# A transformer layer with gathered expert rows: the background work cut into one piece per pair of rows

## What is computed

```
def peer_ffn(hn, wq, subkeys, u, v):
    ...
        q = (xc @ wq).reshape(PEER_CHUNK, PEER_HEADS, 2, PEER_DKEY // 2)
        s = jnp.einsum('chpd,hpkd->chpk', q, subkeys).astype(jnp.float32)
        s1, i1 = lax.top_k(s[:, :, 0], PEER_TOPK)
        s2, i2 = lax.top_k(s[:, :, 1], PEER_TOPK)
        ...
        top, sel = lax.top_k(cand, PEER_TOPK)
        expert = jnp.take_along_axis(cidx, sel, axis=-1)
        g = jax.nn.softmax(top, axis=-1)
        act = jax.nn.gelu(jnp.einsum('cd,chkd->chk', xc, u[expert]).astype(jnp.float32))
        return jnp.einsum('chk,chkd->cd', (g * act).astype(v.dtype), v[expert])
```

## Time and profile before

| | us |
|---|---|
| three runs | 2373.06, 2374.31, 2378.94 |
| their median | 2374.31 |
| the profiled execution: its own time | 2377.95 |
| its span, first to last instruction | 2376.1 |
| of the span: up to the first gather | 722.7 |
| first dot to last dot | 728.8 to 2358.0 |
| mean granted clock of TensorE | 0.796 |

### The profile page before, as it was taken

How to read it: one execution, slowest core, us unless ns; L and a number is a source line. 1 busy time by engine, 2 the same in 40 slices (tenths; PEclk the granted TensorE clock), 3 DMA queues, 4 the chain that set the end, 5 groups by cost and what they waited for, 6 DMA issues and landing times. The chain is left out here.

```text
span 2376.1 us, 24181 instructions
## 1 busy us (share of the span) xinstructions
PE 1642.0 (69%) x8217; PEld 693.9 (29%) x8217; DVE 1360.5 (57%) x4295; ACT 403.7 (17%) x1217; POOL 650.6 (27%) x560
## 2 busy tenths in 40 slices
PE   5999998879794785786366566765664564655564
PEld 2334685535451221433021222431231111111111
DVE  2200026810217667456955675657776989999855
ACT  2000234612311220020101112101110100000101
POOL 0000000000005435423422343232443434444442
PEclk9999978989796897586678787667886757677777
DMA  7211600053009879878888997889999999999996
GB/s 217 71 42 64 205 11 1 3 186 124 36 1 377 355 297 410 354 289 310 316 343 325 381 390 318 354 333 360 393 381 418 396 381 351 395 395 385 391 385 278
DMA packets 124994, 654.73 MB, mean 276 GB/s; under 512 B 22960, under 2 KB 34256, under 8 KB 56928
## 3 DMA queue, kind: packets, MB, share of 16 engines
q0 software_dynamic: 78016, 562.07, 59.4%
q1 hardware_dynamic: 41816, 82.86, 10.2%
q10 hardware_dynamic: 5040, 8.26, 1.0%
HBM read 642.78 MB, written 14.55 MB: 277 GB/s over the span
## 5 line engine op out<-in xcount | busy, mean ns | idle before, releaser
L1362 PE MATMUL row_sum<-arena 64*64 64x512 f32 x4096 | 739.5, 852 | 587.2 <-DVE arena L2324 571.9
L767 POOL DMA_INDIRECT arena<-in_peer_uv,expert x512 | 594.0, 1160 | 1389.4 <-PE row_sum L1362 840.7
L2288 DVE CUSTOM_DVE_ANT_0 arena<-arena 128x1024 f32<-128x1024 f32 x520 | 637.0, 1225 | 333.4 <-DMA arena<-in_peer_uv,expert 322.1
L1362 PEld LDWEIGHTS row_sum<-arena 64*64 64x64 f32 x4096 | 174.3, 175 | 1110.3 <-DVE arena L2324 813.4
L1578 ACT ACTIVATE arena<-arena 128x2 f32<-128x2 f32 x260 | 53.2, 205 | 1135.9 <-DVE arena L2288 1135.3
L816 PE MATMUL bank<-arena 128*128 128x512 f32 (+2 forms) x288 | 119.9, 571 | 0.0
L1781 DVE TENSOR_TENSOR arena<-arena 128x256 f32<-128x256 f32 (+5 forms) x20 | 6.4, 320 | 197.3 <-ACT arena L1439 197.3
L816 PE MATMUL row_sum<-arena 128*128 128x512 f32 (+3 forms) x272 | 109.7, 558 | 0.0
L2307 DVE TENSOR_TENSOR arena<-arena 128x128 f32<-128x128 f32 x256 | 75.1, 293 | 8.4 <-DVE arena L2297 0.4
L1581 ACT ACTIVATE arena<-arena 128x2 f32<-128x2 f32 x260 | 53.3, 205 | 125.7 <-DVE arena L2294 125.6
L2324 DVE SCALAR_TENSOR_TENSOR arena<-arena 128x128 f32<-128x128 f32 x256 | 74.0, 289 | 0.1
(11 more groups left out here) (314 smaller groups left out, 2055.9 us busy)
## 6 DMA issues: line engine op xcount, KB each, us to landing
arena<-in_w_in SPq DMA_DIRECT2D x6, 2048.0 KB, 7.8
arena<-in_w_out SPq DMA_DIRECT2D x2, 4096.0 KB, 24.1
arena<-in_peer_uv,expert POOLq DMA_INDIRECT x512, 9.1
arena<-in_w_mq SPq DMA_DIRECT2D x2, 2048.0 KB, 12.6
arena<-in_peer_wq SPq DMA_DIRECT2D x2, 2048.0 KB, 11.2
arena<-in_w_mo SPq DMA_DIRECT2D x2, 2048.0 KB, 18.9
sc_scores<-arena ACTq DMA_DIRECT2D x4, 1024.0 KB
arena<-in_cache_mem_k SPq DMA_DIRECT2D x2, 2048.0 KB, 11.5
```

The costliest lines, as they stand in the source:

```text
L767: pool.indirect_dma_start(out=ring[k], out_offset=None, in_=a["peer_uv"], in_offset=bass.IndirectOffsetOnAxis(ap=idx, axis=0)).then_inc(ro ...
L1362: ins = pe.matmul(row_sum[r][o * HALF:(o + 1) * HALF, cols], spread[tokens, p % SPREADS, y, :], ring[k][tokens, D + half * 512:D + (half + ...
L2288: return dve.tensor_tensor_reduce(out=ring[k][:, 0:D], in0=ring[k][:, 0:D], in1=other, scale=1.0, scalar=0.0, op0=ALU.mult, op1=ALU.add, a ...
```

## The change

The generators stay, but every piece is given the number of the pair at which it is due, and all three engines call `advance(steps, p)` at each pair.

- On PE the background piece of pair p stands ahead of the value rows of pair p-1, no longer behind them.
- Pieces are cut smaller: one batch-and-group run of page keys per pair, two runs of page values, half a bank of the output projection, one query, one memory-key unit of the sample and so on. The halves of a page-key product and of a value product go to the two column halves of the array (`y`).
- Tile 3 and the sample tokens no longer share memory output, expert queries and scores: tile 3's end at pair 144, the sample's own memory attention follows, and its scores are made at pair 206. For that `w_mo` and the expert query weights `wq` are loaded once more each.
- The sample's eight heads are chosen as one, with (token, head) on 64 partitions, in group 27; the gates and expert numbers are brought into columns through DRAM and not by a transpose on PE.
- The gathers of the page values are issued one pair earlier and wait at pair 31; the retention state's four large DVE instructions are halved; three final norms move to the groups 17, 18 and 26.
- In the front only the order of the key scores changes (the two halves take turns).

The table of pairs and the core of the diff:

```diff
-VALUES_AT = 4
...
-FINAL_SQUARES = {PAIR_AT[H * t + 12, 7]: t for t in range(3)}
-FINAL_NORMS = {PAIR_AT[H * t + 13, 7]: t for t in range(3)}
-SAMPLE_HEADS_AT = 21
+FINAL_SQUARES = {PAIR_AT[n, 1]: t for t, n in enumerate((17, 18, 26))}
+FINAL_NORMS = {PAIR_AT[n, 5]: t for t, n in enumerate((17, 18, 26))}
+SAMPLE_HEADS_AT = 27
...
-    for head in range(H):
-        steps[SAMPLE_HEADS_AT + head].append((SAMPLE, head))
+    steps[SAMPLE_HEADS_AT].append((SAMPLE, 0))
...
-STEP_TURNS = ((1, 1), (2, 2), (3, 3), (4, 4), (5, 5), (6, 10), (7, 20), (8, 21), (9, 23), (10, 24), (11, 27),
-              (12, 28), (13, 29), (14, 30), (15, 35), (16, 38), (17, 39), (18, 42), (19, 44), (20, 45), (21, 46),
-              (22, 47), (23, 48), (24, 49), (25, 55), (26, 56), (27, 57), (28, 64), (29, 65), (30, 68), (31, 76),
-              (32, 77))
-STEPS_DONE = 99
+KEYS_AT, VALUES_AT, KIND_DONE = (14, 54), (41, 67), (51, 73)
+STATE_AT = 75
+OUT_AT = {PT - 1: 91, PT: 95}
+QUERIES_AT = 106
+UNITS_AT = 113
+MEM_OUT_AT = {PT - 1: 126, PT: 189}
+EXPERT_AT = {PT - 1: 134, PT: 196}
+MEM_KEYS_AT = (150, 162)
+MEM_VALUES_AT = (176, 184)
+NORM_COLS = 11
+STEPS_DONE = 999
...
+            sp.wait_ge(mo_done, 2 * PT)
+            sp.dma_start(back.wq, wq).then_inc(wq_in, 16)
+            sp.wait_ge(qp_done, 2 * H)
+            sp.dma_start(w_mo, w_mo_rows).then_inc(mo_in, 16)
+
+            sp.wait_ge(scores_stored, 16 * PT)
+            for piece, (s, v) in enumerate(((qp_done, 2 * H), (m_keyT_done, DB), (m_keyT_done, 2 * DB),
                                             (m_oT_done, PT * HM + 1))):
                 name, b0 = ("cache_mem_k", "cache_mem_v")[piece // 2], 4 * (piece % 2)
                 sp.wait_ge(s, v)
...
+                if t == SAMPLE:
+                    sp.wait_ge(gates_ready, 1)
+                    for dst, src in ((sc_expert, expert_p[0:64, :]), (sc_gate, best_v[0:64, 0:TOPK])):
+                        sp.dma_start(dst.rearrange("b (h k) -> (b h) k", h=H), src).then_inc(scratch_stored, 16)
+                    sp.wait_ge(scratch_stored, 96)
+                    sp.dma_start(expert_s[:, :], sc_expert.rearrange("b s -> s b"), allow_slow_non_contiguous=True).then_inc(idx_ready, 16)
+                    sp.dma_start(half_gate[:, SLOTS:SLOTS + DB], sc_gate.rearrange("b s -> s b"), allow_slow_non_contiguous=True).then_inc(sample_gates_in, 16)
...
-                    pool.wait_ge(idx_ready, 3)
+                    pool.wait_ge(idx_ready, 2 + 16)
                 else:
                     pool.wait_ge(routed, ROUTED[divmod(n, H)])
-                if (n, x) == (VALUES_AT, 0):
+                values_behind = 0 <= p - KEYS_AT[0] - BG - 1 < BG // 2
+                if p == KEYS_AT[0] + BG + 1:
                     pool.wait_ge(s_sc_done, 2)
                 for y in range(2):
                     nth, k = divmod(2 * p + y, RING)
@@ -771,8 +785,8 @@
...
-                    if n == VALUES_AT:
-                        gather_pages(val_rows, "cache_slc_v", val_in[0], 2 * x + y)
+                    if values_behind:
...
                     b = grp.out_bank(n)
                     bank = claim(b)
                     for k in range(KC):
-                        ins = pe.matmul(bank[:, 0:grp.width], grp.w_mq[:, k, hh * P:(hh + 1) * P], grp.hnT[:, k, :],
+                        if k == KC // 2:
+                            yield
+                        ins = pe.matmul(bank[0:R, :], grp.catT[t][:, k, 0:R],
+                                        grp.w_out[:, k, half * 512:(half + 1) * 512],
                                         start=(k == 0), stop=(k == KC - 1))
-                    ins.then_inc(qm_done, 1)
-                    freed[b] = (qm_ready, n + 1)
-                pe.wait_ge(qm_ready, HM * nth)
+                    ins.then_inc(out_done, 1)
+                    freed[b] = (out_added, n + 1)
+                    yield
+
+
+            def memory_query(grp, nth, hh):
+                n = HM * (nth - 1) + hh
...
+                            ins = pe.matmul(banks[2][y * 64:(y + 1) * 64, :], q_mask[0:HD, bg, :], keyT[0:HD, y, :],
+                                            start=(i == 0), stop=(i == len(runs) - 1))
                         return ins
 
-                    for i in range(BG * nc_):
-                        bg, cc = divmod(i, nc_)
-                        if i and i % 4 == 0:
-                            yield 5 + 3 * kind + i / (BG * nc_)
-                        bank = claim(gi % 2)
-                        for q in range(4):
-                            j = 4 * cc + q
-                            ins = pe.transpose(bank[0:HD, q * P:(q + 1) * P], keys[:, bg, j * HD:(j + 1) * HD], ident)
-                        ins.then_inc(s_keyT_done, 1)
-                        freed[gi % 2] = (s_keyT_ready, gi + 1)
+                    for i, run in enumerate(runs):
+                        yield KEYS_AT[kind] + i
                         if i:
-                            key_scores(i - 1, gi - 1)
-                        gi += 1
-                    key_scores(BG * nc_ - 1, gi - 1).then_inc(s_sc_done, 1)
-                    yield 6 + 3 * kind
-                    for cc in range(nc_):
-                        freed[2 + cc] = (s_max, 2 + kind)
+                            key_scores(i - 1)
+                        else:
+                            pe.wait_ge(qmask_ready, 1)
+                            pe.wait_ge(key_in[kind], (16 * BG, 16)[kind])
+                            claim(2)
+                        for y, (bg, j0) in enumerate(run):
+                            bank = claim(y)
+                            for q in range(4):
+                                j = j0 + q
+                                ins = pe.transpose(bank[0:HD, q * P:(q + 1) * P], keys[:, bg, j * HD:(j + 1) * HD], ident)
+                            ins.then_inc(s_keyT_done, 1)
+                            made += 1
+                            freed[y] = (s_keyT_ready, made)
+                    yield KEYS_AT[kind] + len(runs)
+                    key_scores(len(runs) - 1).then_inc(s_sc_done, 1)
+                    freed[2] = (s_max, 2 + kind)
...
-                    pe.wait_ge(val_in[kind], (16 * BG, 16)[kind])
-                    pe.wait_ge(s_pT_ready, 2 + kind)
-                    bank = claim(1)
+                    each = (2, 4)[kind]
                     for bg in range(BG):
-                        for j in range(nj):
-                            ins = pe.matmul(bank[0:HD, bg * R4:(bg + 1) * R4], vals[:, bg, j * HD:(j + 1) * HD],
-                                            s_probsT[:, j, bg * R4:(bg + 1) * R4], start=(j == 0), stop=(j == nj - 1))
+                        if bg % each == 0:
+                            yield VALUES_AT[kind] + bg // each
+                        if bg == 0:
+                            pe.wait_ge(val_in[kind], (16 * BG, 16)[kind])
+                            pe.wait_ge(s_pT_ready, 2 + kind)
+                            claim(1)
+                        for j in range(0, nj, 2):
+                            for y in range(2):
+                                ins = pe.matmul(banks[1][y * HD:(y + 1) * HD, bg * R4:(bg + 1) * R4],
...
+                                                vals[:, bg, (j + y) * HD:(j + y + 1) * HD],
+                                                s_probsT[:, j + y, bg * R4:(bg + 1) * R4], start=(j == 0), stop=(j == nj - 2))
                     ins.then_inc(s_oT_done, 1)
                     freed[1] = (s_oT_ready, 1 + kind)
+                    yield KIND_DONE[kind] - 1
...
+                cat_transposes(3)
+                out3, out_s = (output_projection(back, 2, t) for t in (3, SAMPLE))
+                for i in range(4):
+                    yield OUT_AT[3] + i
+                    next(out3)
+                    if i == 2:
+                        cat_transposes(SAMPLE)
+                for i in range(4):
...
+                yield from memory_rows(3, 2)
+                yield from expert_scores(3, 2)
...
-                key_scores_of(back, SAMPLE)
+                yield from memory_rows(SAMPLE, 3)
+                yield from expert_scores(SAMPLE, 3)
...
 
 
@@ -1379,15 +1434,9 @@
             for b in range(4, 8):
                 claim(b)
             for p, (n, x) in enumerate(PAIRS):
-                if (n, x) == (HEADS - 2, 2):
-                    bank = claim(0)
-                    pe.wait_ge(gates_ready, 1)
-                    pe.transpose(bank[:, 0:DB], expert_f[0:DB, :], ident[0:DB, 0:DB])
-                    pe.transpose(bank[:, DB:2 * DB], gate_t[0:DB, :], ident[0:DB, 0:DB]).then_inc(rt_done, 1)
+                advance(steps, p)
...
-
-            def sample_gates_shifted():
-
-                b3 = best_v[0:DB, :].rearrange("p (h k) -> p h k", h=H)
-                top = col[0:DB, 32:40]
-                order(dve.tensor_copy(top, b3[:, :, 0]))
-                tt(b3, b3, wide(top, DB, H, TOPK), ALU.subtract).then_inc(sample_gate, 1)
 
```

(16 more changed lines are left out.)

632 lines of the change are left out of this document (338 added, 294 removed).

## The result

The changed kernel takes 2287.46 us, the median of 4 runs (2273.87 to 2295.52); beside it the kernel before took 2376.62 us (2373.06 to 2379.31). The ratio is 0.962, 95% interval 0.957 to 0.967: 89 us less, where the prediction said 2276 us and 98 less. The profiled execution took 2289.83 us, its span is 2288.0.

A forecast was written before the change was run, and what follows sets the result against it. Bound: the gathers' bandwidth, with DMA idle behind large background pieces. Loop: gathers 1300, other traffic 134, jitter 49, PE's pieces 30, retention state 15, late loads 5, together 1533 us against 1631; hence 2276 us, range 2232 to 2335.

The forecast's parts named there:

- groups 21 to 28: Late pairs of the loop, sample's heads chosen at one go: 5.2 us a pair, DVE busy about 0.85.
- Late loads: Output weights asked for at about pair 85, wanted by PE at pair 91: 5 us (0 to 10).
- Page and window values: Value pieces on PE, 2.4 us each, 0.8 over the floor in 12 pairs: 10 us (0 to 20).
- The sample's memory values: Eight pieces on PE of 3.45 us, 6.85 with value rows, 1.85 over the floor: 15 us.
- The retention state on DVE: Four large instructions of 20.5 us over eight pairs; DVE needs 55.5 us where DMA needs 40: 15 us.
- Page key pieces at no loss: On PE, 3.1 us a piece, about 2.1 if column halves overlap, 5.1 with value rows: no loss.
- Output quarters: Output projection and memory output on PE, 3.5 us a piece, 5.45 with value rows: 5 us over 12 pairs.
- The added loads: Expert query weights, 4.2 MB, and `w_mo`, 2.1 MB, loaded once more in the loop: 15 us, never free.
- Everyday jitter: 0.19 us over the 5.0 us floor in each of 260 pairs: 49 us (0 to 96).
- The slack of the ring takes it.: At pair 31 POOL waits for the last page-key product, about a pair late; the ring hides this.
- Half the gain by pieces in the ring's way: Rival, chance 0.20: pieces ahead of value rows delay buffer release in some 92 pairs, 46 us more, 2322.
- The lower clock: Rival, chance 0.08 in part or whole: TensorE at 0.50 in the 92 pairs with a large piece, 2507 us.

The follow-up runs named there:

- experiment 2: The changed kernel with all engines' background pieces taken only every second pair, two at once: 2458.64 us; every eighth pair, eight at once: 2578.85 us.
- experiment 1: The changed kernel with TensorE's background piece of pair p again behind the value rows of pair p-1: 2282.53 us, ratio 0.9587 to the kernel before.
- experiment 4: The changed kernel with the sample's page and window values on one column half of TensorE: 2305.72 us, beside 2288.29 of the changed kernel.
- Experiment 6: Three edits of the changed kernel: one more VectorE operation a pair in groups 21 to 27, 2296.07 us; 8.4 MB of unneeded copies, 2318.54; six row buffers, 2487.35.
- e4_fill2: The changed kernel with two unread 128x512 matmuls ahead of the value rows in the background-free pairs of 210 to 247: 2274.81 us, ratio 0.9569.
- e1_behind: The changed kernel with only the order on TensorE undone, background piece behind the value rows: 2282.53 us, ratio 0.9587 to the kernel before.
- e8_onehalf: The changed kernel with page and window values of the sample on one column half instead of two: 2305.72 us.
- experiment 5: The changed kernel with two unread 128x512 matmuls ahead of value rows: in late background-free pairs, 2274.81 us; also in early ones and pairs 176 to 187, 2275.48 us.

## Why the prediction was right, and where it was not

**The mechanism held.** Large pieces of PE stop the release of buffers, the ring holds a few us, the DMA engines idle; cut the pieces and the idle time goes. The prediction named the page values as the longest hole, and the pair that held them went from 30.2 us to 5.3. The same pieces taken by twos and by eights lose 171 and 291 us (experiment 2). Every sign named in advance can be read: the DMA share is 0.97 (0.97 or more was said); the pairs with page values take 5.0 to 6.5 us each (under 7); the longest wait of POOL for PE is 13.5 us (12 was said), at pair 70, behind a late row and not a large piece. Two signs failed: value rows at 2.86 us on the mean, not 2.5, beside a clock that stayed at 0.74; and groups 21 to 28, below. The loop came out at 1547 us in one profiled execution and 1540 in another, against 1533.

**That it came so near is in part luck.** Taking each stretch at 5.19 us a pair, the other traffic that its trace shows at 415 GB/s and the terms of the sum that fall in it, pairs 14 to 39 came out 7 us over, 52 to 87 11 over and 216 to 247 7 over, while 40 to 51 stayed 6 below and 126 to 215 9 below. Of the 11, 7 are a term that the sum does not have: at the end of a tile DVE adds the tile's sums in four operations, 4.97 us in one piece, and PE waits for it.

```profile
1113.31 4.97 DVE L2413 TENSOR_TENSOR arena<-arena,row_sum 64x1024 f32<-64x1024 f32 x4 [0.99 <-PE row_sum L1417]
```

The four pairs there took 27.7 us where 4 × 5.19 are 20.8, and the other tile ends look alike, 28.6 and 30.3; the kernel before has the same (28.9, 26.0, 27.1), so the change neither gains nor loses by it. The late row of pair 70 is in the 11 too. In pairs 126 to 215 the sample's memory values cost less than allowed, below.

**Term by term.**

- *Late loads, 5 us (0 to 10).* PE's wait for the output weights was 5.04 us in one execution and 4.10 in the other. Held, but its cost is larger than the wait: the order of pieces and value rows around it and the 3.7 us pieces behind it are worth 10 us in the profiled executions (experiment 1).
- *Page and window values, 2.4 us a piece (1.6 to 3.2).* 1.10 us when the clock is up and 1.87 when it is down. The halves overlap almost wholly, and the reserve of 10 us was not needed. Without the overlap the kernel was 17 us longer (experiment 4).
- *The sample's memory values, 15 us.* A piece took 1.95 us at the upper clock and 3.57 at the lower, and the eight pairs with them 46.6 us in one execution and 44.1 in the other, 5 and 3 over 8 × 5.19. Too large by 10.
- *The retention state on DVE, 15 us.* Pairs 75 to 83, where its parts stand, took 58.1 us, 11 over 9 × 5.19. Held.
- *Page key pieces at no loss.* Each is 1.08 + 1.06 us at the upper clock, the overlapped value named in the prediction. PE waits for ACT's copies in between, 28.2 us in all, which the step had not looked at; pairs 14 to 23 still took 5.31 us each, so it held.
- *Output quarters, 0.45 us over the floor in 12 pairs.* A piece took 3.70 us as forecast from 3.5, with PE busy 20.00 of 20 us and the share at 0.77. Pairs 88 to 107 took 136 us; by the sum's own terms they are 20 × 5.19 = 104, loads of 4.2, 2.1 and 2.1 MB 20, eight quarters 4 and the late load 5, 133. Right.
- *The added loads, 15 us in proportion to their bytes.* Experiment 6 agrees with the price: 8.4 MB more cost 20 to 23 us where they are, 20 by this rule.
- *Groups 21 to 28 at 5.2 us once the second head is gone.* This step failed. As a whole their 64 pairs, 168 to 231, took 384.5 us, 6.01 a pair with DVE at 0.72, against 353.8 before, since the sample's pieces and 15 MB of other traffic now stand there; only the quiet pairs from 216 on can be compared. I read 5.55 us a pair beside a DVE share of 0.91 and took the one for the cause of the other. The trace of the kernel before already spoke against it. First its pairs 216 to 231, with two heads to a group, then 232 to 247, where one group has one head and the other none:

```profile
2122.00:2209.50 87.50, 47.78 (x256) 10.73 (x256) 79.57 (x284) 7.33 (x37) 39.87 (x33) 0.73 0.98 385
2209.50:2297.10 87.60, 50.73 (x258) 11.51 (x258) 60.54 (x181) 10.79 (x42) 35.73 (x31) 0.69 0.98 389
```

DVE falls from 0.91 to 0.69 and a pair takes 5.47 us in both. In the changed kernel DVE's share of pairs 216 to 247 fell to 131.1/173.0 = 0.76 and a pair still took 5.41 us; an added DVE operation of 20 to 27 us in all cost 0 to 8. The pace there was set by the turn of the ring, at a clock of 0.66. That is 173.0 - 32 × 5.19 = 7 us in these pairs alone, half of the 14 us by which the loop was missed; in the second execution, 170, it is 4 of 7.
- *Everyday jitter of 0.19 us a pair* was taken from 16 pairs at a clock of 0.77 and carried to all. In the quiet stretch what stands over the floor is not jitter but the turn of the ring, 0.41 us a pair, and it depends on how long rows stay on the cores; at the tile ends it is DVE's addition.
- *"The slack of the ring takes it."* The prediction gave the ring a few us of cover. Where pairs run at 5.4 us it has none: a buffer less cost 200 us. Experiment 4, at the page values, paid for 9 to 17 of 19 us.
- *The piece ahead costs nothing because PE waits anyway.* Held for pieces of 1 to 2 us, not for the output projection.

**The rivals.** Half the gain by pieces in the ring's way (2322) did not come, although its mechanism is at work in pairs 88 to 107. The lower clock did not come as a whole, but it is there in part: the value rows did not get faster, and with pieces of 3.6 us PE stayed at 0.50 while busy all the time.

The Trainium skill, "TensorEngine Tiling (Array Packing)", section "Key Properties", says that changing the tiling mode drains TensorE. There are more changes of shape now, and in the timeline the value rows at 830.27 begin before the piece from 829.27 of 1.06 us has ended; the ends of PE's records are modelled, so a drain could hide in some 0.1 us, but no gap is seen here either.

**What stays open.** The parts of the change were not undone one by one. That the sample's heads are chosen as one, that its work no longer shares steps with tile 3's, and where the pieces now stand may each hold a part of the 89 us; that the small pieces are needed for all of it is what experiment 2 shows. Whether the clock acts through the time of the value rows alone is not measured apart: at 0.66 they are 100.50/32 = 3.14 us a pair, at 1.00 they are 62.4/32 = 1.95 (row below, of e4_fill2 in pairs 216 to 247), and the turn became 1.0 us shorter, from 18.9 to 17.9, which fits; but e1_behind came to 5.20 us a pair at 0.74 and e8_onehalf to 5.35 at 0.76. Which way of spreading the output projection is best was not tried.

```profile
L1418 PE MATMUL row_sum<-arena 64*64 64x512 f32 x512 | 62.4, 601 | 38.6 <-DVE arena L2403 38.5
```

## What to carry to other kernels

Work that shares an engine with the release of buffers should be cut until a piece fits into one period; then check the next large piece too, since what one closed hole gives can be lost there. Before giving a pace to a busy engine, look for a stretch where that engine has less to do and see whether the pace moves. Compute the turn (period times buffers) and compare it at two places or with one buffer less: if it stays the same, latency on the ring is the bound, whatever the share of the DMA engines says. Put background behind the work that frees buffers when its input may be late.

## What the runs showed of the hardware

- The busy share of the DMA engines does not tell used bandwidth: 0.98 stood beside 388 GB/s and 1.01 beside 414 for the same gathers. Read GB/s with it.
- TensorE's granted clock stayed at 0.50 through 20 us in which PE was busy 20.00 us with 128x4 products and value rows (experiment 4), and was 1.00 through 163.5 us in which it was busy 123 us with fillers and value rows (experiment 5).
- 128x512 matmuls that nobody reads shortened this kernel: 13 us of 2288 by the medians, with two of them in each of 38 pairs and also in each of 72.
- Products of 128x4 on the two column halves overlap almost wholly: 32 in 1.10 us at the upper clock and 1.87 at the lower, against 2.03 and 3.57 on one half.
